# A decoder trunk on one core: the first norm's squares summed over a stationary block of ones, the diagonal picked by VectorE, and the squares put ahead of the next layer's weight casts

## What is computed

```python
for l in range(DEPTH):                                   # DEPTH = 2
    h = _modulate(_rmsnorm(x), sh1, sc1)                 # the first norm of a layer
    z = h @ w_in[l]                                      # 36 panels of 128 columns
    ...                                                  # three mixers, gates
    x = x + g1[:, None, :] * (merged @ w_o[l])
    h2 = _modulate(_rmsnorm(x), sh2, sc2)                # the second norm
    x = x + g2[:, None, :] * _peer(h2, w_pq[l], sub_keys[l], u_tab[l], v_tab[l])
return _rmsnorm(x, final_norm)                           # the last norm

# _rmsnorm(x) = x * rsqrt(mean(x * x, axis=-1) + EPS) for each token
```

## Time and profile before

| | us |
|---|---|
| median of 3 runs | 3391.51 |
| lowest and highest run | 3388.35, 3396.68 |
| the profiled execution, its own time | 3398.23 |
| its span in the trace | 3396.4 |
| TensorE busy | 3335.4 (98% of the span) |
| VectorE busy | 2685.5 (79%) |
| ScalarE busy | 1400.9 (41%) |
| GpSimd busy | 1451.2 (43%) |
| mean granted clock of TensorE | 0.987 |

### The profile page before, as it was taken

The page is one execution under the profiler, slowest core; times in us unless marked ns, Lnnn a source line. Parts: engine busy times, 40 slices in busy tenths (PEclk is TensorE's granted clock), DMA queues, the critical chain, the costliest instruction groups (busy, mean ns, idle before and its releaser), DMA issues.

```text
span 3396.4 us, 51667 instructions
## 1 busy us (share of the span) xinstructions
PE 3335.4 (98%) x16944; PEld 2905.3 (86%) x16944; DVE 2685.5 (79%) x4905; ACT 1400.9 (41%) x2298; POOL 1451.2 (43%) x1291
## 2 busy tenths in 40 slices
PE   7999999999999999999999999999999999999999
PEld 5777789999999988888877767999999998888887
DVE  6455668999888689999854556799998877899996
ACT  3334343434477433333343342443435773333333
POOL 1011106766662345566301101086767524456661
PEclk9999999999999999999999999999999999999999
DMA  6475437767799999999734744477768999999994
GB/s 228 134 253 187 150 121 221 213 206 230 228 309 327 349 393 378 399 404 402 304 129 148 241 158 154 144 221 215 214 205 260 337 320 379 361 405 399 405 400 184
DMA packets 306395, 909.86 MB, mean 268 GB/s; under 512 B 69076, under 2 KB 101892, under 8 KB 305316
## 3 DMA queue, kind: packets, MB, share of 16 engines
q0 software_dynamic: 163792, 473.58, 40.6%
q1 hardware_dynamic: 105552, 383.83, 31.8%
q10 hardware_dynamic: 36868, 50.35, 4.1%
HBM read 792.14 MB, written 115.47 MB: 267 GB/s over the span
## 4 chain that ended last, share of the span: by engine, by line
PE 91%; DVE 4%; DMA 2%; issue 1%; POOL 1%; ACT 1%; ACTq 0%; SPq 0%; DVEq 0%; POOLq 0%
PE ps L462 15%; PE ps L464 15%; PE ps L463 15%; PE ps L1076 11%; PE ps L1074 10%; PE ps L1075 10%; PE ps L1054 3%; PE ps L877 2%; PE ps L974 1%; PE ps L975 1%; PE ps L976 1%; PE ps L933 1%; PE ps L506 1%; PE ps L1014 1%; DVE urow L1693 1%
## 5 line engine op out<-in xcount | busy, mean ns | idle before, releaser
L462 PE MATMUL ps<-mov,whl 128*128 128x384 f32 (+1 forms) x2816 | 1007.7, 358 | 1.2 <-DVE whl L449 1.2
L464 PE MATMUL ps<-mov,whl 128*128 128x384 f32 (+1 forms) x2816 | 987.6, 351 | 0.0
L463 PE MATMUL ps<-mov,whl 128*128 128x384 f32 (+1 forms) x2816 | 987.0, 350 | 0.0
L449 DVE TENSOR_TENSOR whl<-raw,whl 128x1024 fp32r<-128x1024 f32 x648 | 792.0, 1223 | 183.3 <-ACT whl L439 178.7
L439 ACT CAST whl<-raw 128x1024 fp32r<-128x1024 f32 x648 | 680.1, 1050 | 100.5 <-ACT hst L1241 96.4
L1074 PE MATMUL ps<-whl,wgthl 128*128 128x512 f32 x1536 | 607.9, 396 | 2.2 <-DVE wgthl L1792 2.2
L1076 PE MATMUL ps<-whl,wgthl 128*128 128x512 f32 x1536 | 609.0, 397 | 0.0
L1075 PE MATMUL ps<-whl,wgthl 128*128 128x512 f32 x1536 | 603.7, 393 | 0.0
L462 PEld LDWEIGHTS ps<-mov,whl 128*128 128x128 f32 x2816 | 530.4, 188 | 39.4 <-issue 8.7
L464 PEld LDWEIGHTS ps<-mov,whl 128*128 128x128 f32 x2816 | 529.5, 188 | 31.6
L463 PEld LDWEIGHTS ps<-mov,whl 128*128 128x128 f32 x2816 | 530.2, 188 | 30.4 <-issue 2.2
(11 more groups left out here) (263 smaller groups left out, 3628.4 us busy)
## 6 DMA issues: line engine op xcount, KB each, us to landing
raw<-in_uT_tab SPq DMA_DIRECT2D x256, 512.0 KB, 4.1
raw<-in_v_tab SPq DMA_DIRECT2D x256, 512.0 KB, 6.8
expert_spill<-hst ACTq DMA_DIRECT2D x256, 192.0 KB
hin<-expert_spill POOLq DMA_DIRECT2D x256, 192.0 KB, 7.8
gt<-weight_spill POOLq DMA_DIRECT2D x64, 768.0 KB, 9.1
raw<-in_w_in SPq DMA_DIRECT2D x72, 512.0 KB, 11.4
raw<-in_w_mod SPq DMA_DIRECT2D x64, 512.0 KB, 3.7
weight_spill<-stage POOLq DMA_DIRECT2D x14, 2048.0 KB, 14.8
```

Source lines behind the costliest of these rows:

```text
L449: nc.vector.tensor_tensor(whl[:, m % RING, 1], raw[:, raw_n(m) % RAW], whl[:, m % RING, 0].bitcast(F32), ALU.subtract).then_inc(lo_done, 1)
L462: nc.tensor.matmul(o, w[:, 0, k], src[:, 0, k, :cols], start=(k == 0), stop=False)
L463: nc.tensor.matmul(o, w[:, 0, k], src[:, 1, k, :cols], start=False, stop=False)
L464: mm = nc.tensor.matmul(o, w[:, 1, k], src[:, 0, k, :cols], start=False, stop=(k == KC - 1))
```

## The change

It does four things. `first_squares` sums with the ones stationary. A new function of VectorE, `own_sums`, multiplies the 128 x 512 sums by the identity repeated four times and sums each block of 128 columns, which leaves the same 128 x 4 block as before; the root of the first and last norm is taken from it. On ScalarE, the eight squares between the layers come ahead of the two casts. On VectorE, the two low parts come behind the reciprocal, and at the start `own_sums` stands between columns 0 to 3 and columns 4 and 5.

```diff
@@ first_squares (TensorE)
-            pe.wait_ge(sq_ready, l * SQ_ALL + SQ_H1 + q + 1)
-            token_squares(pe, sq[:, q % 2], 2, q == 0, q == KC - 1).then_inc(sq_used, 1)
+            sum_squares(pe, l, SQ_H1 + q, 2, q == 0, q == KC - 1)
+
+    def own_sums(dve, l):
+
+        dve.wait_ge(sq_used, 1 + l * SQ_ALL + SQ_H1 + KC)
+        of_all = root[:].rearrange("p (t c) -> p t c", t=TT)
+        nc.vector.tensor_tensor(of_all, ps[:, 2].rearrange("p (t c) -> p t c", t=TT),
+                                ident[:].unsqueeze(1).to_broadcast([P, TT, P]), ALU.mult).then_inc(own_picked, 1)
+        dve.wait_ge(own_picked, l + 1)
+        nc.vector.tensor_reduce(ss4[:], of_all, AX, ALU.add).then_inc(own_summed, 1)
@@ take_root (ScalarE)
+        if k == 0:
+            act.wait_ge(own_summed, l + 1)
         if k in (0, 3):
-            nc.scalar.activation(rt4[:], ps[:, SSQ_BANK[k], :TT], ACT.Sqrt, bias=eps[:], scale=1.0 / width
-                                 ).then_inc(root_ready, 1)
+            sums = ss4[:] if k == 0 else ps[:, SSQ_BANK[k], :TT]
+            nc.scalar.activation(rt4[:], sums, ACT.Sqrt, bias=eps[:], scale=1.0 / width).then_inc(root_ready, 1)
@@ norm_h (ScalarE)
                 warm_root(act)
+                for q in range(KC):
+                    act.wait_ge(x_added, l * KC + q + 1)
+                    square(act, l, SQ_H1 + q, x_sb[:, q])
                 if l:
                     split_hi(act, l, 0)
                     split_hi(act, l, 1)
-                for q in range(KC):
-                    act.wait_ge(x_added, l * KC + q + 1)
-                    square(act, l, SQ_H1 + q, x_sb[:, q])
             take_root(act, l, 3 * which, D)
@@ norm_h (VectorE)
+            if not (l or which):
+                first_columns(0, KC // 2)
+            if not which:
+                own_sums(dve, l)
+            if not (l or which):
+                first_columns(KC // 2, KC - 2)
+            rstd4(dve, l, 3 * which)
             if l and not which:
                 split_lo(dve, l, 0)
                 split_lo(dve, l, 1)
-            if not (l or which):
-                first_columns(0, KC - 2)
-            rstd4(dve, l, 3 * which)
             dve.wait_ge(root_spread, l * 2 + which + 1)
@@ the last norm (VectorE)
+        own_sums(dve, DEPTH)
         rstd4(dve, DEPTH, 0)
```

More of the change, by code:

```diff
@@ L259, in build_trunk @@
     rt4 = sb("rt4", [P, TT])
+    ss4 = sb("ss4", [P, TT])
     rinv4 = sb("rinv4", [P, TT])
@@ L386, in build_trunk @@
     sq_ready, sq_used = sem("sq_ready"), sem("sq_used")
+    own_picked, own_summed = sem("own_picked"), sem("own_summed")
     root_ready, rstd_ready, root_spread = sem("root_ready"), sem("rstd_ready"), sem("root_spread")
```

## The result

| | before | changed |
|---|---|---|
| median, us | 3394.99 (5 runs, 3388.35 to 3398.5) | 3366.47 (5 runs, 3362.24 to 3367.42) |
| ratio | | 0.992 [0.9907, 0.9933] |
| profiled execution, its span | 3398.23, 3396.4 | 3366.47, 3364.7 |
| mean granted clock | 0.987 | 0.991 |

The change saves 28.5 us (0.8%), three times the forecast; the interval of the ratio allows 23 to 32 us. 3366.47 lies outside the range given. Eight to ten of these microseconds are the predicted ones. The others come from a place that the change does not seem to touch.

The account below looks back on a forecast made before the run. The prediction took TensorE to bound the kernel (91% of the span). It summed 6.1 us between the layers, 3.5 at the last norm and 0 at the start to 9.6, giving 3382 us, range 3377 to 3390.

Parts of the forecast that it names:

- something unseen: Anywhere: the chance of 0.05 left for an outcome that neither the forecast nor any named rival covers.
- (1): Between the layers: a chunk summed with ones stationary takes 0.86 us at full clock, against 0.89; the swap gives only the clock.
- rival B: In the norms: sums of 512 columns do not hold the clock; 3.7 us more, time 3395; chance 0.08.
- (2): Between the layers: squares no longer wait for the casts, so the first sum starts at 1701.35 instead of 1702.47.
- (3): Between the layers: sums done at 1708.5, 5.9 us won so far; the two casts run under other work and cost nothing.
- (4): Between the layers: VectorE's two new operations add 1.45 us (1.35 to 1.6) to the path; root 4.5 us earlier.
- (5): Between the layers: root and reciprocal done at 1710.45, spread about 1.2 us at full clock, first product 4.3 us earlier.
- (6): Between the layers: the gemm starts 5.7 us earlier, with up to 0.4 more from the code fetch; taken as 6.1.
- rival A: After the sums: the clock falls in TensorE's new pause; gain 7.5 us, time 3384; chance 0.30.
- The last norm: At the end: root 2.7 us earlier and spread at full clock 0.85 more, 3.5 us won.
- The start: First norm: sums end before VectorE needs them and its additions fit into idle time for DMA; 0 us.
- rival C: At the start: the sums hold the clock but wake it too late; 1.7 us lost, time 3384; chance 0.07.

Follow-up runs that it names:

- x1: The kernel before with one unused 32-byte tile where the change puts its new tile, nothing else computed: 3374.63 us, ratio 0.9951.
- x6: The kernel before with 32 unused bytes just ahead of `wgthl`, moving it and the tiles behind it to multiples of 64: 3379.02 us, ratio 0.9961.
- x9: The change with 32 unused bytes ahead of `wgthl`, moving it back off the multiple of 64: 3378.62 us, 12.2 us more than the change.
- x5: The kernel before with an unused tile of 64 bytes instead of 32: 3390.29 us, ratio 0.9997.
- x7: The change with `fin` and `lbase` put behind `rinv4`, so that the two identities start at a multiple of 64: 3368.2 us, ratio 0.9931 to the kernel before.
- x4: The kernel before with only the new order of casts and low parts, squares still stationary, old addresses kept: 3388.67 us, ratio 0.9992.
- x10: The kernel before with 32 unused bytes ahead of `whl`, so `whl` is off a multiple of 64 and tiles behind it on: 3402.07 us, ratio 1.0029.
- x2: The whole change with `ss4` in place of an unused 32-byte tile, so other tiles keep the addresses of before: 3382.5 us, ratio 0.997 to the kernel before.
- x3: The kernel before with only the ones stationary and `own_sums`, old order of casts and low parts, old addresses: 3383.81 us, ratio 0.9977.
- x8: The change with 8 idle matmuls of 512 columns in TensorE's pause between sums and spread: 3367.53 us, ratio 0.9929 to the kernel before.

## Why the prediction was wrong

**The step that failed is the sum itself**, "Total: 6.1 + 3.5 + 0 = 9.6", where 28.5 were measured, and with it the count of what the change does. It priced every instruction and every order, and gave the new tile no price at all. The 0.05 for "something unseen" was the only place for it, and the range was built from the errors of the terms that I had. What was missing is 17.8 us (x1). Of it, 13.0 us are x1's value loops (11.6 in the change), and they follow the place of `wgthl` (x6, x9). The output panels' three lines give about 2.4 us of busy time. The other 2.4 us I could not place: single profiles differ by more than that, since the first value loop starts at 1159.0 before and at 1153.5 in x5, which gained nothing.

The value loop could have given more. Where nothing waits, 42 passes through its three lines took 29.40 us before (3340.15 to 3369.55), and 25 passes 17.17 in the change (3323.51 to 3340.68): 0.2333 and 0.2289 us a matmul, which would be 20 us for 4608. But TensorE now waits 8.1 us for `wgthl` at line 1086 instead of 2.2. The chain of waits says what stands behind that; of the kernel before and, below, of the change, by line:

```profile
PE ps L462 15%; PE ps L464 15%; PE ps L463 15%; PE ps L1076 11%; PE ps L1074 10%; PE ps L1075 10%; PE ps L1054 3%; PE ps L877 2%; PE ps L974 1%; PE ps L975 1%; PE ps L976 1%; PE ps L933 1%; PE ps L506 1%; PE ps L1014 1%; DVE urow L1693 1%
```

```profile
PE ps L464 15%; PE ps L466 15%; PE ps L465 15%; PE ps L1087 7%; PE ps L1086 7%; PE ps L1088 7%; DMA hin<-expert_spill 6%; PE ps L1066 2%; PE ps L889 2%; POOL weight_spill L768 1%; DVE whl L451 1%; DVE otok L1796 1%; PE ps L986 1%; PE ps L945 1%; PE ps L987 1%
```

The value loop's three lines fall from 31% of the span to 21%, and the load of `hin`, from which `wgthl` is made, comes in with 6%. The DMA share of 1.01 in the stretches, before and after, says that the DMA engines were busy throughout already. A loop that TensorE bounded has come to the edge of its loads. That a still faster TensorE would gain little there follows from this, but no run tested it.

The norm, by the prediction's own steps:

- **(1) Pace of a chunk, 0.86 to 0.87 us at full clock.** Nearly right: eight chunks take 7.60 us, 0.95 each, since the squares' gaps alternate between 0.23 and 0.41 us; why they do is not shown. Clock 1.00 in the sums, so **rival B** is out.
- **(2) Sums without a wait.** Right: the first sum is 3.49 us behind the first transpose, forecast 3.64.
- **(3) Sums done.** VectorE starts at +11.13, forecast 10.8: 0.5 us later by the 0.95 a chunk, less the 0.15 of step (2). The casts (1.97 us) end under VectorE's work and cost nothing.
- **(4) VectorE's two operations.** 0.69 + 0.69 us, 1.51 with the hand-overs; forecast 1.45. Root at +12.64, forecast 12.2.
- **(5), (6) Spread and gemm.** Here **rival A** came about between the layers, by the sign it was given: a `keep_busy` row over 3.5 us (4.26). The spread took 2.04 us instead of 1.2, and the gemm came 4.0 us earlier, not 5.7 (A: 4.4). In x7 and x9 the same pause did not lower the clock, so A is a matter of the execution. The first product was 0.3 us later than forecast, since the low parts were done at 1702.79 and the spread just before. Against the loss at the gemm's start stands the 1.47 us of "issue" time: the prediction counted on at most 0.4 of it, and all of it is gone (that it was a fetch of code is not shown). So 5.6 us are won at the next projection, near the 6.1 forecast, because two errors cancel, which is luck.
- **The last norm.** Root at +9.14, forecast 8.6, again through 0.95 a chunk. The clock held over the pause, and 2.8 us were won, forecast 3.5. The "before" of this term depends on the execution too: the old sums took 11.22 us in the earlier trace rows, but 9.22 in x1 and 8.97 in x5, where the clock fell later. From the first of the last transposes to the end, the six profiles with the old sums (before, x1, x4, x5, x6, x10) took 24.8 us on average and the six with the new ones 22.7, so 2.1 us is the better figure.
- **The start.** 0 us, as forecast: **rival C** did not come about.

Together 8.4 us by this pair of profiles and 9.9 by the runs of x2 (6.8 to 13.2) are what the prediction's 9.6 stood for. Its mechanism, the clock held by the sums of 512 columns and the wait for the casts gone, was right; its size was right partly by the luck told above. The swap did not lose some 5 us a norm: x3 is 8.6 us faster. The page "TensorE: Matmul & The Clock Gate" of the Trainium skill (Back-to-back issue gap) gives the figures from which that loss was worked out for a single matmul by itself, and says in the same section that in a stream of loads and matmuls both set the spacing. The rows agree with the latter. A record of one column took 0.11 us at full clock (0.89 for eight), as long as a transpose of 128 columns (3.65 for 32), so the columns moved did not set the pace, and at the lower clock the weight loads were busy for 9.31 of 9.40 us.

## What to carry to other kernels

A change that declares even a small tile moves all that is declared behind it. Work out where each operand of TensorE falls within 64 bytes, before and after, and time the old kernel with the padding alone beside the change, or the change will be credited with what its padding does. And in a loop that TensorE bounds, look at how close the loads already are, since that can cap what a faster operand gives.

## What the runs showed of the hardware

- **An operand of TensorE that lies 32 bytes off slows matmuls of 512 columns.** Off means 32 above a multiple of 64, counted from `x_sb`. In the value loop, where nothing waits, a matmul took 0.2333 us in the traces with one operand off (before, x2, x5, x9, x10) and 0.2289 in those with both on (the change, x1, x6, x7), at a clock of 1.00. It shows for the stationary operand (`wgthl`: x6, x9) and for the moving one (`mrg`: fast in x1 and x9, slow in x2 and x6; `whl` in the value loop: x10). A shift of 64 bytes changes nothing (x5). For the identity as an operand nothing was seen (x7). What does this inside the engine or the memory is open; no other offsets within 64 bytes were tried.
- **It does not show for every matmul.** With 384 columns the pace stayed at 0.173 us (x10). The tiles above are declared `F32R`, one record a matmul. Plain float32 matmuls (two records) did not change when both their operands moved from off to on, as these groups show, before and changed:

```profile
L877 PE MATMUL ps<-ukv,lat 128*128 128x512 f32 x64 | 28.8, 592 | 0.0
```

```profile
L889 PE MATMUL ps<-ukv,lat 128*128 128x512 f32 x64 | 28.8, 592 | 0.0
```

- **A pause of 2.20 us is followed by either clock.** Behind the same pause, with the same work ahead of it, the spread took 2.04 us between the layers in the change, 2.05 in x2, 1.43 in x3 (casts first there) and 1.13 in x7 and x9. At the end it took 1.33, 1.13, 1.13, 1.87 and 1.13 in these five. With eight throwaway matmuls in the pause it took 1.13 in both places, in the one profile of x8.
